# Paged sample attention moved into the stage of the prompt's attention

## What is computed

```python
cum = jnp.cumsum(logf, axis=1)
s = einsum('bqhe,bkhe->bhqk', q, k) * SCALE + cum[q] - cum[k]     # causal mask
out = softmax(s) @ v
```

```python
past = kv_pool[page_table]                       # 8 x 32 pages, 256 KB each
suffix = reverse_cumsum(lf_past) - lf_past
s_past = einsum('bthe,bshe->bhts', q, past_k) * SCALE + suffix + logf_new
s_new  = q . k_new * SCALE
p = softmax([s_past, s_new]);  out = p[past] @ past_v + p[new] * v_new
```

## Time and profile before

| | us |
|---|---|
| median of 3 runs (4083.2 to 4088.5) | 4086.03 |
| the profiled execution's own time | 4071.64 |
| its span, first to last instruction | 4069.9 |
| `fox_prompt`, first to last instruction | 774.5 to 1116.6 |
| `fox_decode`, first to last instruction | 1823.1 to 2126.2 |

### The profile page before, as it was taken

The page is one execution under the profiler, slowest core; times in us unless marked ns, Lnnn a source line. Parts: engine busy times, 40 slices in busy tenths (PEclk is TensorE's granted clock), DMA queues, the critical chain, the costliest instruction groups (busy, mean ns, idle before and its releaser), DMA issues. The chain is left out here.

```text
span 4069.9 us, 48077 instructions
## 1 busy us (share of the span) xinstructions
PE 3246.7 (80%) x16937; PEld 2731.4 (67%) x16937; DVE 1618.9 (40%) x2794; ACT 818.9 (20%) x1434; POOL 508.0 (12%) x346
## 2 busy tenths in 40 slices
PE   4799599599966788403556968999999959999997
PEld 3688499488745577301115757989989847878786
DVE  2122122244333344346643334544545444444444
ACT  2111111133333222100002222211212121212121
POOL 0000000100011122100002202211212021212120
PEclk8899799799966699756778989999999979999999
DMA  6322422231022111237734443110101051111111
GB/s 249 157 90 100 165 92 81 56 58 34 9 71 63 51 44 42 95 88 286 281 126 135 144 164 116 42 52 31 62 31 42 5 198 41 52 41 52 42 42 47
DMA packets 208583, 363.80 MB, mean 89 GB/s; under 512 B 89327, under 2 KB 127912, under 8 KB 202522
## 3 DMA queue, kind: packets, MB, share of 16 engines
q1 hardware_dynamic: 150035, 229.65, 17.8%
q10 hardware_dynamic: 54464, 101.24, 6.7%
q0 software_dynamic: 4016, 32.05, 2.4%
HBM read 296.55 MB, written 95.49 MB: 96 GB/s over the span
## 5 line engine op out<-in xcount | busy, mean ns | idle before, releaser
L2000 PE MATMUL cm_g_ps<-cm_h_hi,cm_up_hi 128*128 128x344 f32 (+1 forms) x880 | 309.6, 352 | 123.1 <-POOL cm_up_lo L1839 91.0
L2001 PE MATMUL cm_g_ps<-cm_h_lo,cm_up_hi 128*128 128x344 f32 (+1 forms) x880 | 307.4, 349 | 0.0
L2002 PE MATMUL cm_g_ps<-cm_h_hi,cm_up_lo 128*128 128x344 f32 (+1 forms) x880 | 307.3, 349 | 0.0
L2000 PE MATMUL cm_u_ps<-cm_h_hi,cm_up_hi 128*128 128x344 f32 (+1 forms) x880 | 307.0, 349 | 0.0
L2002 PE MATMUL cm_u_ps<-cm_h_hi,cm_up_lo 128*128 128x344 f32 (+1 forms) x880 | 305.6, 347 | 0.0
L2001 PE MATMUL cm_u_ps<-cm_h_lo,cm_up_hi 128*128 128x344 f32 (+1 forms) x880 | 305.6, 347 | 0.0
L2000 PEld LDWEIGHTS cm_g_ps<-cm_h_hi,cm_up_hi 128*128 128x128 f32 x880 | 166.5, 189 | 145.5 <-issue 131.9
L288 PE MATMUL pja_acc<-pja_w_hi,pja_h_hi 128*128 128x480 f32 (+1 forms) x512 | 198.4, 387 | 61.0 <-DVE pja_h_lo L225 61.0
L1839 POOL TENSOR_TENSOR cm_up_lo<-cm_up_raw,cm_up_hi 128x2048 fp32r<-128x2048 f32 x44 | 204.2, 4641 | 285.7 <-ACT cm_up_hi L1861 285.7
L2544 PE MATMUL fd_o_ps<-fd_kv,fd_p 128*4 128x256 f32 x512 | 130.6, 423 | 131.7 <-ACT fd_p_own L2432 131.7
L1844 POOL TENSOR_TENSOR cm_dn_lo<-cm_dn_raw,cm_dn_hi 128x1024 fp32r<-128x1024 f32 x44 | 107.7, 2467 | 995.4 <-ACT cm_dn_hi L1876 995.4
(11 more groups left out here) (418 smaller groups left out, 7101.9 us busy)
## 6 DMA issues: line engine op xcount, KB each, us to landing
cm_up_raw<-in_w_up SPq DMA_DIRECT2D x44, 1024.0 KB, 4.8
fd_kv<-in_fox_kv ACTq DMA_DIRECT2D x128, 256.0 KB, 6.2
fd_kv<-in_fox_kv SPq DMA_DIRECT2D x128, 256.0 KB, 6.4
cm_dn_raw<-in_w_down SPq DMA_DIRECT2D x44, 512.0 KB, 3.5
out_s_win<-in_cache POOLq DMA_DIRECT2D x1, 16376.0 KB, 32.4
proj_a<-pja_row ACTq DMA_DIRECT2D x17, 962.0 KB, 3.9
proj_b<-pjb_row ACTq DMA_DIRECT2D x17, 643.0 KB, 3.3
sp_raw<-proj_b SPq DMA_DIRECT2D x16, 640.0 KB, 4.1
```

The costliest lines, as they stand in the source:

```text
L2000: pe.matmul(out, hi, h_hi[:, k, cs], start=(k == 0), stop=False)
L2001: pe.matmul(out, hi, h_lo[:, k, cs], start=False, stop=False)
L2002: last = pe.matmul(out, lo, h_hi[:, k, cs], start=False, stop=(k == KT - 1))
```

## The change

`fox_decode` is gone as a stage. Its work is written into the instruction lists of `fox_prompt`, now `fox_stage`, as generators that each engine's list resumes at given steps (`Beside`). The 160 steps are numbered through, and token b's work is tied to them: step `10 + 17*b + s`.

- Keys: POOL, no longer DVE, multiplies four pages (a "quart") by the query, at s = 0, 2, .. 14; DVE sums each quart one step later (`gather`), s = 1, 3, .. 15.
- s = 17: DVE bias and maximum. s = 18: POOL's `partition_all_reduce`. s = 22: DVE subtracts. s = 23: ACT exponentials. s = 24 to 31: PE's value product of one quart in each step; its four pages go to four column groups, PSUM partitions 0, 32, 64 and 96, and are summed at the end. s = 34: DVE keeps the diagonal parts.
- Pages: SP alone loads them, into a ring of 11 quarts, each freed by its value product.
- To make room in PSUM, `z_ps` and `o_ps` have one bank instead of two; the parts of q are made per block (`("q", b+2)` two steps before a block's end), those of k and the bias row one per step. To make room in SBUF, q is held for three blocks.
- The loads of q, k, v and the stores of the prompt's output are issued by ACT.

```diff
+    def token_slot(b, step):
+        return 10 + 17 * b + step
 ...
+    def until(self, slot):
+        while self.next_slot is not None and self.next_slot <= slot:
+            self.next_slot = next(self.steps, None)
 ...
-        o_ps = ps("o", [P, 2, QB])
-        z_ps = ps("z", [P, 2, QB])
+        o_ps = ps("o", [P, QB])
+        z_ps = ps("z", [P, QB])
+        e_ps = ps("e", [P, 2, QB])
 ...
         def _(sp):
+            for n in range(NQ):
+                if n == 8:
+                    sp.wait_ge(setup_done, 1)
+                if n >= RING:
+                    sp.wait_ge(freed, n - RING + 1)
+                for g in range(QUART):
+                    page = sp.value_load(table[0:1, at:at + 1], ...)
+                    sp.dma_start(kv[:, n % RING * QUART + g]..., kv_d[bass.ds(page, 1)]...).then_inc(page_landed[n % RING], 16)
 ...
+        def decode_pool(pool):
+            def product(b, k):
+                n = b * QUARTS + k
+                pool.wait_ge(page_landed[n % RING], 16 * QUART * (n // RING + 1))
+                if n >= 2:
+                    pool.wait_ge(reduced, n - 1)
+                pool.tensor_tensor(prod[:, n % 2], kv[:, at:at + QUART, 0],
+                                   q_own[:, b:b + 1].to_broadcast([P, QUART, F]), ALU.mult).then_inc(multiplied, 1)
+            for b in range(DEC):
+                for k in range(QUARTS):
+                    yield token_slot(b, 2 * k)
+                    product(b, k)
+                yield token_slot(b, 18)
+                pool.wait_ge(top_ready, b + 1)
+                pool.tensor_tensor(idle[:, 1:2], idle[:, 0:1], idle[:, 0:1], ALU.add)
+                pool.partition_all_reduce(m_dec[:, b % 2], top_dec[:, b % 2], P, RMAX).then_inc(md_ready, 1)
 ...
+        def decode_vector(v):
+            def gather(b, k):
+                n = b * QUARTS + k
+                v.wait_ge(multiplied, n + 1)
+                v.reduce_sum(s_dec[...], prod[:, n % 2]..., AX.X).then_inc(reduced, 1)
+            for slot in range(token_slot(0, 0), token_slot(DEC, 18)):
+                yield slot
+                for b in range(DEC):
+                    at = slot - token_slot(b, 0)
+                    if at in range(1, 2 * QUARTS, 2):
+                        gather(b, at // 2)
+                    if at == 17:
+                        maximum(b)
+                    if at == 22:
+                        shifted(b)
+                    if at == 24:
+                        sums(b)
+                    if at == 34:
+                        keep(b)
 ...
+        def decode_tensor(pe):
+            def attend(b, k):
+                if k == 0:
+                    pe.wait_ge(rest_ready, 1)
+                    pe.wait_ge(p_ready, b + 1)
+                    if b:
+                        pe.wait_ge(o_read, b)
+                for g in range(QUART):
+                    page, c = k * QUART + g, g % COLS
+                    last = pe.matmul(e_ps[32 * c:32 * c + H, 0, 0:F], p_dec[:, x, :, page],
+                                     kv[:, n % RING * QUART + g, 1], start=(page < COLS), ...)
+                last.then_inc(freed, 1)
 ...
             for b in range(NBLK):
                 for i in range(size[b]):
+                    beside.until(first[b] + i)
                     for n in scores_at.get((b, i), []):
                         maximum(b + 1, n)
 ...
-        fox_prompt(nc, pa, i["consts"], gates, mb)
+        fox_stage(nc, pa, i["consts"], gates, mb, i["table"], ...)
 ...
-        fox_decode(nc, pa, i["consts"], i["table"], ...)
```

More of the change, by code:

```diff
@@ L566, in normalise @@
                                 ALU.mult).then_inc(o_ready, 1)
-            for g in range(4):
-                for k in range(3):
-                    low(0, g, k)
+            for part in parts_first:
+                low(*part)
             for n in range(size[0]):
@@ L578, in _ @@
                         normalise(b - 1)
-                    for p in parts_at.get((b, i), []):
-                        low(*p)
+                    for part in parts_at.get((b, i), []):
+                        low(*part)
             normalise(NBLK - 1)
+            beside.until(SLOTS + 100)
+            v.wait_ge(sums_mm, 1)
+            dve.link(v, v.reciprocal(rden_dec[:].rearrange("p b h -> p (b h)"), e_ps[0:1, 1, 0:DEC * H]))
+            for k, bank in enumerate((s_ps[0:1, 0], s_ps[0:1, 1], t_ps[0:1, 0], t_ps[0:1, 1])):
+                last = v.tensor_tensor(out_dec[:, 2 * k:2 * k + 2].rearrange("p b (h e) -> p (b h) e", e=HD),
+                                       bank.rearrange("p (h e) -> p h e", e=HD),
+                                       rden_dec[:, 2 * k:2 * k + 2].rearrange("p b h -> p (b h)").unsqueeze(2)
+                                       .to_broadcast([1, 2 * H, HD]), ALU.mult)
@@ new lines, in head, with load_twice, high @@
+            def head(col, h):
+                return pa[P:, col + h * HD:col + (h + 1) * HD].rearrange("(t p) e -> p t e", p=P)
+            def load_twice(tile, col, h, landed):
+                for c in range(2):
+                    act.dma_start(tile[:, :, c], head(col, h)).then_inc(landed, 16)
+            def high(kind, *at):
+                act.wait_ge(part_turned, part_no[kind, *at])
+                if kind == "q":
+                    r = at[0] % 3
+                    act.activation(q_both[0:HD, r], z_ps[0:HD], ACT.Copy, scale=SCALE)
+                    last = act.activation(q_more[HD:P, r], z_ps[HD:P], ACT.Copy, scale=SCALE)
+                else:
+                    x, cs = at[0] % 2, slice(at[1] * QB, (at[1] + 1) * QB)
+                    if kind == "k":
+                        last = act.activation(k_both[:, x, cs], z_ps[:], ACT.Copy)
+                    else:
+                        last = act.activation(k_more[0:AUG, x, cs], z_ps[0:AUG], ACT.Copy)
@@ L735, in _ @@
                     value(b, i)
+            beside.until(SLOTS + 100)
+            pe.wait_ge(o_read, DEC)
+            pe.wait_ge(o_ready, NBLK)
+            pe.wait_ge(p_ready, DEC)
+            pe.matmul(e_ps[0:1, 1, 0:DEC * H], consts[:, ONES, 0:1], den_dec[:].rearrange("p b h -> p (b h)"),
+                      start=True, stop=True)
+            for k, bank in enumerate((s_ps[0:1, 0], s_ps[0:1, 1], t_ps[0:1, 0], t_ps[0:1, 1])):
+                last = pe.matmul(bank, consts[:, ONES, 0:1], o_heads[:, 2 * k:2 * k + 2].rearrange("p b c -> p (b c)"),
+                                 start=True, stop=True)
+            last.then_inc(sums_mm, 1)
 BIAS_ROW = 384
```

630 lines of the change are left out of this document (295 added, 335 removed).

## The result

| | before | after |
|---|---|---|
| median of 5 runs, us | 4085.0 (4076.0 to 4088.5) | 4125.2 (4109.9 to 4137.3) |
| profiled execution, us | 4071.6 | 4132.8 |
| its span, us | 4069.9 | 4131.0 |
| mean granted clock over the span | 0.895 | 0.873 |
| attention stage of the prompt, us | 344.8 | 704.2 |

The changed kernel is **slower by 1.0%**: ratio 1.0101, 95% interval 1.0071 to 1.0131. The forecast was 4071, some 15 us faster. In the profiled executions the merged stage takes 359.4 us more than the prompt's stage did, and 305.2 us of the separate stage are saved, which makes +54 us of the 61 by which the two spans differ. The medians differ by 40 only: the profiled execution of before is faster than all five of its runs, that of after the second slowest of five.

A forecast was written before the change was run, and what follows sets the result against it. PE was taken to bound `fox_prompt`, busy 282 of 294 us; added terms of 290 us against the 305 saved gave -15 us, hence 4071 us, with 8 in 10 between 4000 and 4125.

The forecast's parts named there:

- value product: PE's products of four pages: 1.07 us a quart, 48 quarts counted, +51 us (bounds +21 and +82).
- other PE work: On PE, own-value products, transposes and suffix sums at the start, last sums and divisions: +14 us together.
- clock: PE after waits of 6 us and more: 2.9 us lost at 12 to 13 of 14 waits, +36 us (0 to +41).
- wait for the maximum: GpSimd's code changes around each all-reduce delay the next key product; PE waits 14.5 us for seven tokens, +101 us.
- ring: Token b+1's fourth quart waits for a buffer freed by token b's first value product: 6 us for 7 tokens, +42.
- `z_ps`, `o_ps`, gathers, start: Single `z_ps` bank +27 us, `o_ps` nothing, DVE's gathers beside the maxima +16, loads sharing DMA engines at the start +3.
- the waits are longer, and PE stays at the low clock through whole tokens: Rival: page landings at the median 6.3 us and low clock through whole tokens, +24 and 7 x 5, 4130 us; chance 0.09.
- all four side by side: Rival on PE's value products: four column groups run together, 0.43 us a quart, -46 us, 4040 us; chance 0.15.
- serial groups: Rival on PE's value products: column groups run one after the other, 1.71 us a quart, 4102 us; chance 0.27.
- one code change only: Rival: GpSimd changes code once per token, or the way back is hidden, -63 us, 4023 us; chance 0.12.
- The start: Loads of q and k share the DMA engines with 8 MB of pages at the stage's start: +3 us (-5 to +10).

The follow-up runs named there:

- e5: Changed kernel with the all-reduce replaced by a copy and only the first 11 quarts loaded and reread, output not the reference's: 3897.9 us.
- e1: Changed kernel with GpSimd's all-reduce replaced by a copy of each partition's own maximum, output not the reference's: 4036.7 us.
- e9: Changed kernel with the maximum over partitions made on PE and DVE, without GpSimd's all-reduce: 4005.9 us, 0.9833 of before.
- e2: Changed kernel with GpSimd issuing the next token's first two key products ahead of the all-reduce: 4040.3 us, 0.9902 of before.
- e7: Changed kernel with SP issuing no page load before the prompt's first k has landed: 4125.3 us, 1.0113 of before.
- e11: Changed kernel with four extra matmuls on constants before the last block's first value step: 4105.9 us, 1.0075 of before.
- e8: Changed kernel with 14 extra matmuls on constants at step 19 of tokens 0 to 6, where PE stood idle: 4114.3 us, 1.0090 of before.
- e4: Changed kernel with a ring of 12 quarts instead of 11: 4046.8 us.
- c2: Changed kernel with maximum on PE and DVE, 12-quart ring, page loads behind first k, other slots, DVE set-up spread: 3905.3 us, 0.9579 of before.

## Why the prediction was wrong, by its own steps

| step | forecast us | measured in the profile us | from |
|---|---|---|---|
| value product | +51 | +35 | 64 quarts x 0.55, at the full clock |
| other PE work | +14 | +11 to +19 | rest of PE busy in after and in e5 |
| clock | +36 | +103 to +111 | below |
| wait for the maximum | +101 | +96.5 | 7 waits of 11.3 to 15.2; 100 in e1 and e9 |
| ring | +42 | +47.5 | 6 waits of 6.2 to 9.0 |
| `z_ps`, `o_ps`, gathers, start | +46 | +58 | rest of PE idle |
| sum | +290 | +359 | stage windows |

**The step that failed is "The clock", mis-sized by a factor of three.** It let 12 to 13 waits bring 2.9 us each. PE's busy time grew by 157 us, of which the value products bring 35. The windows of 1 us put the low clock at 119 us lost for 8 before, +111, and leave 11 for the other PE work. e5 gives the other end: 386.2 less its own 30 lost is 357, against 303 in the same count before, and 54 less 35 leaves 19 for the other work and 103 for the clock. e5 removes the waits and 81 us of PE's busy time go, with the instructions unchanged; the rest is what such a stage pays at its start and behind small waits.

Two things were wrong in the step. It took the length of a restart from the earlier trace rows, 5.8 us. The other eight of `fox_decode` took 3 to 6 us of work too, but that work is a run of products that follow each other without a break; among the prompt's steps a restart took 25 us at 954 to 980 and 50 us at the end. And it counted only waits of 6 us and more, 12 to 13 of them, where the clock is low in 25 stretches: a wait of 2.48 us had 20 us at 0.50 behind it. Why some restarts took 5 us and others 20 to 50, in steps of the same kind, no run shows.

With the other terms as they were, 111 for 36 gives 4146, and with 35 for the value product 4130, near the 4125 measured and on the other side of zero. That this comes so near is partly luck: the sum is then 349 where the profile has 359, the rest of the program adds 7, and both are offset by medians that differ by 21 us less than the profiled executions. The rival "the waits are longer, and PE stays at the low clock through whole tokens" named the right mechanism in its second half and came out at 4130, but by luck as well: its 24 us for late pages weren't there (the ring came out 5.5 above the forecast), and its 7 x 5 us for the clock were again taken from short restarts, where 75 were missing. It had 0.09.

**The value product** was over-estimated. It is 0.55 us a quart at the full clock (0.96 at the low one), near the lower bound of 0.43, so the rival "all four side by side" was right about the unit and the rival of serial groups is out as a cause. The drain at a change of tiling mode, which the Trainium skill names ("TensorEngine Tiling (Array Packing)", Tiling Modes), would then be 0.55 - 0.43 = 0.12 us at most for both changes of a quart, an estimate from that bound; no run separates it.

**The wait for the maximum** was right in place, order and size: 14.5 x 7 forecast, 96.5 measured, both changes of code seen at 6.4 and 7.3 us. The rival "one code change only" is out. It was the largest term and was known beforehand; e2 shows that three lines of order would have avoided most of it.

**The ring** was right too: 6 us forecast, 8 measured, in six of seven tokens.

**`z_ps`, `o_ps` and the gathers.** "`o_ps` costs nothing: DVE normalises in the step before it is needed" was wrong. In DVE's list the decode steps of a slot come first, and the gather of that slot waited for GpSimd. PE waits 3.46 us, and the low clock behind it costs some 22 us. The step looked at when the normalisation is issued, and not at what is queued in front of it. Two sums beside it don't come out as they are written: 2.6 - 2.33 is 0.27 us a step and not 0.5, so the gathers had +9 and not +16, and 2.2 less a short step of 1.36 is 0.8 us and not 1.1, so `z_ps` had 4 us too much. Both made the sum larger and hid part of the error.

**The start** was +3 and is +16: the first score comes at 821.23, before at

```profile
805.51 0.45 PE L670 MATMUL fp_s<-fp_k_both,fp_q_both 128*128 128x128 f32 x1
```

I had named the shared DMA engines and put +10 as the upper end. e7 takes 14.8 of it back with one wait on SP.

**The range** ended at 4125, with the measured median of 4125.2 on its edge. Bounding the clock at +41 is what cut it: that bound multiplied the same short restart.

## What to carry to other kernels

Price a wait on PE with the low clock behind it, and don't bound that price by restarts in work of another kind: the nine of `fox_decode` took 3 to 6 us, and some among the prompt's steps 20 to 50. Here the waits cost 144 us by themselves and some 80 more in PE's speed. When an engine's list mixes a library operation of GpSimd with ordinary ones, ask what stands right behind it: moving two products ahead of it was worth 2% (e2 against after). And before merging two stages, check for every producer of the host stage what may now be queued in front of it, since a side task that waits for data holds up everything behind it in the list.

## What the runs showed of the hardware that I had not expected

**A clock that can stay low under full load.** The same last steps run at 1.00 when the clock was high before them (e5, e11) and at 0.50 for some 51 us when it had fallen (after, and the 64 us stretches of e1, e2, e7 and e9). In e8 and e4 it was low in these steps too, and came back within 7 us. What decides between the two is open.

**A DVE operation can wait for a GpSimd instruction in full.** From c2, GpSimd's product, then two DVE steps beside it:

```profile
1017.96 0.27 DVE L644 TENSOR_REDUCE fp_m_row<-fp_e 4x1 f32<-4x128 f32 x1
1018.02 2.38 POOL L591 TENSOR_TENSOR fp_prod<-fp_kv,fp_q_own 128x1024 f32<-128x1024 f32 x1 [2.13 <-DMA fp_kv<-in_fox_kv]
1018.26 2.15 DVE L645 TENSOR_SCALAR fp_m_diag<-fp_consts,fp_m_row 4x4 f32<-4x4 f32 x1
```

and all eight of that multiplication of 16 numbers:

```profile
L645 DVE TENSOR_SCALAR fp_m_diag<-fp_consts,fp_m_row x8: 217/872/3691, 878.6 to 1200.4; 4x4 f32<-4x4 f32 x8
```

It takes 0.22 us (four of eight) or ends with the product: 1018.26 + 2.15 = 1020.41, 1018.02 + 2.38 = 1020.40. The longest, 3.69 us, ends with the second of two products in a row. The gathers and the maxima of the prompt, which are reductions, take 1.22 and 0.69 us whether a product runs beside them or not. The Trainium skill says so ("SBUF — State Buffer", Who interferes with whom): the pair of SBUF ports that the two engines share is held for a whole instruction, `tensor_scalar` can ask for it and `tensor_reduce` doesn't. In the changed kernel the few such operations met a product seldom (`fp_top`, L790: 0.17 us, once 0.82), so this was no part of the loss.

**Medians and profiles.** The spread of the kernels with many waits is wide (e8 from 4096 to 4131, after from 4110 to 4137, before from 4076 to 4089). The mean clock over the span moves with it (0.890 in e2's fastest execution, 0.876 in its slowest). Where it falls and recovers in each of them one profile can't show; the stages above are each one execution's.
